# Softmax sums of a whole attention stage in one tile, with one reciprocal, one turn and one store per stage, and a block's rows asked for ahead of its weights

## The chip, the core and the metric

One core of a Trainium2 chip runs the whole program. The metric is the device time of one execution in microseconds (us), the median of several runs. Engines in this text: PE is TensorE, DVE is VectorE, ACT is ScalarE, POOL is GpSimd, and SP is the sync engine, whose queue issues most of the DMA transfers here.

## What is computed

Two transformer blocks of two layers each run one after the other, on 1024 tokens with a model width of 1024 (the first block has 256 context tokens beside them). Almost all of the reference lies outside the change. What matters is softmax attention with heads of 64 values, and the projection that mixes all heads:

```python
def one_block(qi):                                  # the other attentions have this form too
    s = jnp.einsum('bqgrd,bsgd->bgrqs', qi, keys).astype(jnp.float32)
    p = jax.nn.softmax(s, axis=-1).astype(vals.dtype)
    return jnp.einsum('bgrqs,bsgd->bqgrd', p, vals)
...
mixed = jnp.concatenate([_merge(out_fox), _merge(out_sb), _merge(out_mla), _merge(out_mem)], axis=-1)
y = jnp.einsum('bsc,cd->bsd', mixed * jax.nn.silu(gate), w_out[l])
h_res = _layer_norm_2(DEEPNORM_ALPHA_2 * h_res + y, ln_g[l], ln_b[l])
```

The first block's attention has 6 heads over all tokens and 4 heads over a neighbourhood with a bias. The second block's has 4 heads with a forget term (causal), 4 with longer queries and keys (causal), and 4 over a memory of 256 tokens.

## The kernel before

The program is a row of stages, each an own block of instructions for all engines; a stage begins when every engine has ended the one before it. Each of the four layers has an attention stage (`attention`) and, behind it, a stage that mixes and projects (`mixed_out`). They hand data over in DRAM: `YCM` holds the heads' outputs before they are divided by their softmax sums (channels by tokens), `RCP` holds one divided by those sums (heads by tokens).

**attention.** The work is cut into groups: one head and up to four blocks of 128 queries. A group passes through these steps: PE multiplies queries by keys into PSUM (`an_s`, lines 2582 to 2592); DVE adds the mask and takes the row maximum (`an_p`, L2727); ACT takes the exponential in place and leaves the row sum in `total` (L2653); PE turns the probabilities (`an_t`, L2600) and DVE or ACT copies them to SBUF (L2738, L2660); PE weighs the values (`an_oacc`, L2628); DVE takes the reciprocal of the group's sums (L2744) and copies the output (`an_oT`, L2745); SP stores both. The sums lie along the partitions, queries down, so the store of a group's reciprocals to `RCP` (L2548) writes 4 x 128 pieces of four bytes each, one for every partition and query block (2 x 128 in a group of two query blocks). There are 98 groups in the four stages (30, 20, 24, 24), 88 of them with four query blocks and 10 with two.

Every engine works through a list of its own in a fixed order. The class `Order` makes the lists: it places each step by a table of estimated costs and needs. On SP's list the loads of a head's queries (`an_q`, L2517), keys (`an_k`, L2526) and values (`an_vT`, L2529) stand between the groups' stores. DVE's list has a step `prep` for each head (L2710, L2711) that rounds keys and queries; it waits until the head's loads have landed, and all of DVE's later steps wait behind it. The last thing on SP's list is a wait for the last stores (L2551).

**mixed_out.** For each block of 128 tokens, `load(t)` on SP's list asks for the rows of `YCM`, `RCP` (spread over 64 partitions, L2820), the gates, and the residual rows. POOL multiplies rows by reciprocals (`divided`, L2902), ACT and DVE apply the gate (L2856, L2976, L2981), ACT rounds (L2865), POOL takes the rest that rounding leaves (`lower`, L2907), PE multiplies by the weights (L2960 to L2962 for the first block of tokens, L2948 to L2950 for the others), and DVE, POOL and ACT add the residual and normalise. The weights come in four parts of 1 MB (L2836), each rounded by ACT (L2878) and split by DVE (L3017). ACT's list begins

```python
weights(0)
tanh(0)
upper(0)
for k in range(1, NK // 2):
    weights(k)
```

and DVE's list begins with its share of `weights(0)`, then `gated(0)`. SP asks for `weights(0)` first, waits until POOL has set `mo_rcp` to one (`whole`, L2921), and then runs `load(0)`. In block two, where two of the eight tiles of 128 channels need no division, `divided` multiplies all eight.

Of the kernel before, what the change touches and what calls it, by code (L numbers as in the profile page):

```python
# [22 lines left out]
ALU = mybir.AluOpType  # L23
# [3 lines left out]
P = 128  # L27
DM = 1024
# [2206 lines left out]
class Order:  # L2235
# [49 lines left out]
    def parts(self):  # L2285
# [17 lines left out]
        for m, x in enumerate(self.scores):  # L2303
# [9 lines left out]
            work["exp", x] = ({"ACT": 0.42 + 0.0009 * w}, [("max", x)] + ([("out", n - 4)] if n >= 4 else []), 0.1)  # L2313
# [73 lines left out]
def attention(core, heads, kvs):  # L2387
# [31 lines left out]
    tg, pv, oo = core.counter("an_p_turned"), core.counter("an_pv"), core.counter("an_o_out")  # L2419
    given_back = {"ACT": core.counter("an_given_act"), "DVE": core.counter("an_given_dve")}  # L2420
    with ExitStack() as s:
# [12 lines left out]
        total = core.sb(s, "an_sum", [P, 4, 4])  # L2434
        rcp = core.sb(s, "an_rcp", [P, NOUT, 4])
# [56 lines left out]

        def stores_of(n):

            return 1 + min(2, len(spec[n]))

        def stored_to(n):

            return 16 * sum(stores_of(i) for i in range(n % NOUT, n + 1, NOUT))
# [5 lines left out]
        with nc.Block() as block:  # L2505

            @block.sync
            def _(sp):
                sp.wait_ge(zeroed.sem, zeroed.nth(3))
                for kind, x in o.on["SP"]:  # L2510
# [28 lines left out]
                    if kind == "store":  # L2539
# [7 lines left out]
                        with nc.allow_non_contiguous_dma(reason="a vector across partitions"):  # L2547
                            sp.dma_start(core.t["RCP"][row // HD, first:first + k * P].rearrange("(j p) -> p j", p=P), rcp[:, u, 0:k]) \  # L2548
                                .then_inc(stored[u].sem, 16)
                for n in range(max(0, NG - NOUT), NG):  # L2550
                    sp.wait_ge(stored[n % NOUT].sem, stored[n % NOUT].after(0) + stored_to(n))  # L2551

            @block.tensor
            def _(pe):
# [10 lines left out]
                for kind, x in o.on["PE"]:  # L2565
# [45 lines left out]
                    if kind == "weigh":  # L2611
# [18 lines left out]
                        ins.then_inc(pv.sem, 1)  # L2630

            @block.scalar
            def _(act):
                for kind, x in o.on["ACT"]:
# [11 lines left out]
                    if kind == "exp":  # L2646
# [46 lines left out]
            def _(dve):  # L2693
# [5 lines left out]
                for kind, x in o.on["DVE"]:  # L2699
# [39 lines left out]
                    if kind == "out":  # L2739
# [4 lines left out]
                        V_.reciprocal(rcp[:, u, 0:k], total[:, n % 4, 0:k])  # L2744
                        V_.tensor_copy(OT[:, u, 0:(k + 1) // 2 * P], O[:, 0:(k + 1) // 2 * P]).then_inc(oo.sem, 1)  # L2745
    counts = [(zeroed, 3), (hi, len(heads)), (lo, len(heads)), (lk, sum(opens)), (au, aug_no[-1]), (vt, vturns_to(len(kvs) - 1)), (qk, NS), (mxs, NS), (mx, NS),
              (ex, NS), (tg, len(o.turns)), (pv, len(o.weighs)), (oo, NG), (neg, int(any_bias)), (given_back["ACT"], o.given["ACT"]),
# [987 lines left out]
```

## Time and profile before

| | us |
|---|---|
| median of 3 runs | 4927.67 (4921.95 to 4930.57) |
| the profiled execution: its own time | 4925.49 |
| its span, first to last instruction | 4923.5 |
| PE busy / DVE busy | 4045.0 / 2709.8 |
| ACT busy / POOL busy | 1538.9 / 1588.0 |
| mean granted TensorE clock | 0.91 of full |
| DMA packets, and of them under 512 B | 621770, 200252 |

Busy times overlap, since the engines run beside each other. A "wait" below is time in which an engine had nothing to do, put down to what ended it. The start of a stage can be seen by its first instructions: the attention stages begin at 1040.35, 2554.95, 3596.94 and 4515.24 us, the stages that mix at 1448.61, 2930.94, 3880.47 and 4798.47 us.

### The profile page before, as it was taken

How to read it: one execution, taken by the hardware profiler on the slowest of the kernel's cores; microseconds unless marked ns; L12 is line 12 of the kernel's file. 1: busy time of each engine (PE TensorE's matmuls, PEld its weight loads, DVE VectorE, ACT ScalarE, POOL GpSimd, SP SyncE). 2: the span in 40 equal slices, each digit the busy share in tenths (PEclk: the TensorE clock that was granted, in tenths of full speed). 3: DMA queues.
4: the chain of work that ended last, by engine and by line, in shares of the span. 5: the costliest groups of instructions: out<-in, count | busy, mean ns of one | idle time of the engine just before them, and what ended most of it. 6: DMA issues, size and time to landing. Idle time of an engine off the chain costs nothing. (4 is left out here: it accounts for less than half of the span.)

```text
span 4923.5 us, 106002 instructions
## 1 busy us (share of the span) xinstructions
PE 4045.0 (82%) x44120; PEld 3163.1 (64%) x44120; DVE 2709.8 (55%) x4560; ACT 1538.9 (31%) x2705; POOL 1588.0 (32%) x1248
## 2 busy tenths in 40 slices
PE   6999788868878899879868877798777679968667
PEld 4887688735556677678846656686345468844446
DVE  3464455455547366545555546755644475566446
ACT  1232233234432133223225432201453320035432
POOL 2232244310016333244411105752321255413115
PEclk8999899979989899999989888799888789989889
DMA  6455433252445545543342446333134643331447
GB/s 192 145 196 189 128 80 87 69 205 33 68 105 163 167 168 190 185 107 80 80 146 45 66 93 194 121 106 114 58 63 47 145 145 115 101 116 41 54 41 204
DMA packets 621770, 572.40 MB, mean 116 GB/s; under 512 B 200252, under 2 KB 519516, under 8 KB 619284
## 3 DMA queue, kind: packets, MB, share of 16 engines
q1 hardware_dynamic: 493780, 488.22, 37.2%
q10 hardware_dynamic: 127616, 78.95, 5.6%
q8 instruction: 265, 4.34, 0.4%
q14 instruction: 109, 0.89, 0.1%
HBM read 378.80 MB, written 192.42 MB: 116 GB/s over the span
## 5 line engine op out<-in xcount | busy, mean ns | idle before, releaser
L1096 PE MATMUL pr_acc<-hH,pr_wh 128*128 128x512 f32 (+1 forms) x1288 | 483.1, 375 | 0.0
L1097 PE MATMUL pr_acc<-hL,pr_wh 128*128 128x512 f32 (+1 forms) x1288 | 466.1, 362 | 0.0
L1098 PE MATMUL pr_acc<-hH,pr_wl 128*128 128x512 f32 (+1 forms) x1288 | 466.0, 362 | 0.0
L2653 ACT ACTIVATE an_p<-an_p,an_stat 128x1280 f32<-128x1280 f32 (+5 forms) x372 | 339.7, 914 | 286.6 <-DVE an_stat L2731 274.7
L2600 PE MATMUL an_t<-ident,an_p 128*128 128x128 f32 x2152 | 331.1, 292 | 88.1 <-DVE an_pT L2738 51.6
L2686 POOL TENSOR_TENSOR an_kl<-an_k,an_kh 128x1280 fp32r<-128x1280 f32 (+3 forms) x36 | 78.5, 2180 | 1003.2 <-DVE an_qh L2711 1003.2
L2600 PEld LDWEIGHTS an_t<-ident,an_p 128*128 128x128 f32 x2152 | 252.6, 148 | 165.9 <-DVE an_pT L2738 59.0
L2628 PE MATMUL an_oacc<-an_pT,an_v 128*64 128x256 f32 (+1 forms) x2352 | 311.1, 391 | 42.1 <-DVE an_oT L2745 19.4
L2727 DVE CUSTOM_DVE_ANT_0 an_p<-an_s,an_mask 128x256 f32<-128x256 f32 (+8 forms) x308 | 275.0, 893 | 114.1 <-PE an_s L2583 63.9
L1465 POOL TENSOR_TENSOR sp_sl<-sp_w,sp_sh 128x512 fp32r<-128x512 f32 x172 | 246.2, 1438 | 200.0 <-DVE sp_sh L1540 181.6
L2004 DVE TENSOR_TENSOR rk_tu<-rk_tu,rk_ps 128x512 f32<-128x512 f32 x300 | 188.9, 683 | 194.4 <-PE rk_ps L1828 194.4
L1140 POOL TENSOR_TENSOR pr_wl<-pr_w,pr_wh 128x1024 fp32r<-128x1024 f32 x58 | 142.9, 2463 | 471.0 <-DVE pr_wh L1160 471.0
L2065 POOL TENSOR_TENSOR rk_ml<-rk_g,rk_lmask 128x256 f32<-128x256 f32 x300 | 211.0, 731 | 257.6 <-PE rk_ps L1814 256.7
L1374 PE MATMUL sp_acc<-sp_ch,sp_sh 128*128 128x512 f32 x728 | 285.8, 393 | 7.6 <-POOL sp_sl L1465 7.6
L1375 PE MATMUL sp_acc<-sp_cl,sp_sh 128*128 128x512 f32 x728 | 285.3, 392 | 0.0
L1376 PE MATMUL sp_acc<-sp_ch,sp_sl 128*128 128x512 f32 x728 | 285.1, 392 | 0.0
L1096 PEld LDWEIGHTS pr_acc<-hH,pr_wh 128*128 128x128 f32 x1288 | 246.2, 191 | 57.8 <-issue 20.7
L2660 ACT COPY an_pT<-an_t 128x512 f32<-128x512 f32 (+3 forms) x348 | 180.7, 534 | 322.3 <-PE an_t L2600 314.5
L2738 DVE COPY an_pT<-an_t 128x512 f32<-128x512 f32 (+3 forms) x264 | 163.3, 626 | 204.3 <-PE an_t L2600 198.3
L1097 PEld LDWEIGHTS pr_acc<-hL,pr_wh 128*128 128x128 f32 x1288 | 245.9, 191 | 38.1 <-issue 1.2
L1098 PEld LDWEIGHTS pr_acc<-hH,pr_wl 128*128 128x128 f32 x1288 | 245.0, 190 | 38.0
L2582 PE MATMUL an_s<-an_kh,an_qh 128*128 128x256 f32 (+2 forms) x564 | 208.1, 379 | 62.6 <-DVE an_stat L2731 46.5
(376 smaller groups left out, 9894.3 us busy)
## 6 DMA issues: line engine op xcount, KB each, us to landing
CHK<-ri_out SPq DMA_DIRECT2D x24, 1920.0 KB, 8.1
rk_in<-CHK SPq DMA_DIRECT2D x240, 128.0 KB, 2.4
pr_w<-in_w_in ACTq DMA_DIRECT2D x58, 512.0 KB, 4.3
UT<-pr_out SPq DMA_DIRECT2D x45, 640.0 KB, 4.6
sp_w<-in_w_in ACTq DMA_DIRECT2D x50, 512.0 KB, 5.2
U<-sp_c SPq DMA_DIRECT2D x100, 256.0 KB, 2.0
mod_w<-in_w_mod SPq DMA_DIRECT2D x16, 1024.0 KB, 8.3
mo_w<-in_w_out SPq DMA_DIRECT2D x16, 1024.0 KB, 9.0
```

Of the source, the lines that this page charges most:

```text
L1096: nc.tensor.matmul(out, wh[:, u, k, 0:m], hi, start=(k == 0), stop=False)
L1097: nc.tensor.matmul(out, wh[:, u, k, 0:m], lo, start=False, stop=False)
L1098: ins = nc.tensor.matmul(out, wl[:, u, k, 0:m], hi, start=False, stop=(k == KT - 1))
L1374: nc.tensor.matmul(to, sH[:, a, k, :], cH[:, i, k, :], start=(k == 0), stop=False)
L1375: nc.tensor.matmul(to, sH[:, a, k, :], cL[:, i, k, :], start=False, stop=False)
L1376: ins = nc.tensor.matmul(to, sL[:, a, k, :], cH[:, i, k, :], start=False, stop=(k == H - 1))
L1465: g.tensor_tensor(sL[:, slot(q, i)], weight(q, i), sH[:, slot(q, i)], ALU.subtract).then_inc(w_lo.sem, 1)
L2065: return nc.gpsimd.tensor_tensor(out, G[:, b % 2, g, :, :, 0, :], lm[:, :, lv:lv + 1, :].to_broadcast([P, 2, 2, CH]), ALU.mult)
L2600: ins = nc.tensor.transpose(bank[:, j * P:(j + 1) * P], Pm[:, n % NPM, j, col:col + P], ident[:])
L2628: ins = nc.tensor.matmul(to, V[:, c % 2, blocks[n][k], :], by_query(PT[:, buffer(n, k), :], a)[:, part, :], start=(k == 0), stop=(k == len ...
L2653: nc.scalar.activation(row, row, ACT.Exp, bias=stat[:, n % NPM, j, 1:2], scale=heads[groups[n][0]].scale, accum_out=total[:, n % 4, j:j + ...
L2727: V_.tensor_tensor_reduce(out=Pm[:, n % NPM, j, 0:width], in0=scores_at(m, width), in1=extra, scale=1.0, scalar=-3.0e38, op0=ALU.add, op1= ...
```

## The change

In `attention`, `total` becomes one tile with a column for every head and query block of the stage (NT columns: 100 and 80 in the first block's two layers, 96 in the second block's). ACT's exponential writes its sum there, and no longer waits for the output copy of four groups earlier. The reciprocal and the store of each group go. At the end of the stage DVE takes one reciprocal of the whole tile, PE turns it to NT x 128, DVE copies it out of PSUM, and SP stores NT rows of 512 bytes to `RCP`, which now has a row for each head in the order of the stage. In `mixed_out`, the setting to one goes, with SP's wait for it; `load(0)` is asked for ahead of `weights(0)`; and `divided` multiplies the tiles that have sums alone, in one instruction for each range of them.

```diff
-            work["exp", x] = ({"ACT": 0.42 + 0.0009 * w}, [("max", x)] + ([("out", n - 4)] if n >= 4 else []), 0.1)
+            work["exp", x] = ({"ACT": 0.42 + 0.0009 * w}, [("max", x)] , 0.1)
...
-        total = core.sb(s, "an_sum", [P, 4, 4])
-        rcp = core.sb(s, "an_rcp", [P, NOUT, 4])
+        q_first = min(sp_[0][0] for sp_ in spec)
+        NT = len(heads) * (TT // P - q_first if any_bias else SEQ // P)
+        total, rcp, rcpT = core.sb(s, "an_sum", [P, NT]), core.sb(s, "an_rcp", [P, NT]), core.sb(s, "an_rcpT", [NT, P])
...
+        def sum_column(n, j):
+            return groups[n][0] * (NT // len(heads)) + spec[n][j][0] - q_first
...
         def stores_of(n):
-            return 1 + min(2, len(spec[n]))
+            return min(2, len(spec[n]))
...
-                        with nc.allow_non_contiguous_dma(reason="a vector across partitions"):
-                            sp.dma_start(core.t["RCP"][row // HD, first:first + k * P].rearrange("(j p) -> p j", p=P), rcp[:, u, 0:k]) \
-                                .then_inc(stored[u].sem, 16)
+                sp.wait_ge(rc.sem, rc.nth(3))
+                sp.dma_start(core.t["RCP"][0:len(heads), q_first * P:q_first * P + NT // len(heads) * P], rcpT[:]) \
+                    .then_inc(sums_out.sem, 16)
...
+                sp.wait_ge(sums_out.sem, sums_out.after(1))
...
+                pe.wait_ge(rc.sem, rc.nth(1))
+                eng, count = o.back[o.uses[-2]]
+                pe.wait_ge(given_back[eng].sem, given_back[eng].nth(count))
+                nc.tensor.transpose(T2[0:NT, len(o.uses) % 2 * 512:len(o.uses) % 2 * 512 + P], rcp[:], ident[:]).then_inc(rc.sem, 1)
...
-                        if n >= 4:
-                            act.wait_ge(oo.sem, oo.nth(n - 3))
-                                             accum_out=total[:, n % 4, j:j + 1]).then_inc(ex.sem, 1)
+                                             accum_out=total[:, sum_column(n, j):sum_column(n, j) + 1]).then_inc(ex.sem, 1)
...
-                        V_.reciprocal(rcp[:, u, 0:k], total[:, n % 4, 0:k])
                         V_.tensor_copy(OT[:, u, 0:(k + 1) // 2 * P], O[:, 0:(k + 1) // 2 * P]).then_inc(oo.sem, 1)
+                dve.wait_ge(ex.sem, ex.nth(NS))
+                V_.reciprocal(rcp[:], total[:]).then_inc(rc.sem, 1)
+                dve.wait_ge(rc.sem, rc.nth(2))
+                V_.tensor_copy(rcpT[:], T2[0:NT, len(o.uses) % 2 * 512:len(o.uses) % 2 * 512 + P]).then_inc(rc.sem, 1)
...
+                load(0)
                 weights(0)
-                sp.wait_ge(whole.sem, whole.nth(1))
-                load(0)
...
-                    nc.gpsimd.tensor_tensor(yt_in[:, u], yt_in[:, u], rb[:, u], ALU.mult).then_inc(yn.sem, 1)
+                    for j0, j1, _ in summed_tiles:
+                        ins = nc.gpsimd.tensor_tensor(yt_in[:, u, j0:j1], yt_in[:, u, j0:j1], rb[:, u, j0:j1], ALU.mult)
+                    ins.then_inc(yn.sem, 1)
...
-                nc.gpsimd.memset(rb[:], 1.0).then_inc(whole.sem, 1)
...
-                  lambda tok: dst[at(tok, P), :], T["U2"], [(0, 2), (4, 8)])
+                  lambda tok: dst[at(tok, P), :], T["U2"], [(0, 2, 0), (4, 8, 4)])
```

Apart from what is added and taken away, every engine's list stands in the order in which it stood. The first place is on SP's list in the first attention stage, where the seventh head's loads stand behind three groups' stores (`an_q`, `an_k`, `an_vT`: queries, keys, values; `YCM<-an_oT`: outputs; `RCP<-an_rcp`: reciprocals). Before:

```order
L2546 DMA YCM<-an_oT 64x2x128
L2546 DMA YCM<-an_oT 64x256
L2548 DMA RCP<-an_rcp 128x4x1
L2546 DMA YCM<-an_oT 64x128 x2
L2548 DMA RCP<-an_rcp 128x2x1
L2517 DMA an_q<-UT 64x1280 x2
L2526 DMA an_k<-UT 64x1280 x2
L2529 DMA an_vT<-UT 64x1280
```

And now:

```order
L2552 DMA YCM<-an_oT 64x2x128
L2552 DMA YCM<-an_oT 64x256
L2552 DMA YCM<-an_oT 64x128 x2
L2523 DMA an_q<-UT 64x1280 x2
L2532 DMA an_k<-UT 64x1280 x2
L2535 DMA an_vT<-UT 64x1280
```

The loads now stand behind the stores of outputs alone; this repeats at each head of all four stages. The second place is the end of the same stage and the start of `mixed_out` on SP's list (`mo_w`: weights, `mo_ycm`, `mo_rcp`, `mo_gate`, `mo_yT`, `mo_x`: what `load(0)` asks for). Before:

```order
L2546 DMA YCM<-an_oT 64x256
L2548 DMA RCP<-an_rcp 128x4x1
L2505 UNCONDITIONAL_BRANCH
L2810 UNCONDITIONAL_BRANCH
L2836 DMA mo_w<-in_w_out 128x2x1024
L2816 DMA mo_ycm<-YCM 128x5x128
L2820 DMA mo_rcp<-RCP 64x5x128 x2
L2823 DMA mo_gate<-UT 128x3x128
L2823 DMA mo_gate<-UT 128x2x128
L2829 DMA mo_yT<-YG 128x3x128
L2833 DMA mo_x<-in_XC 128x1024
L2836 DMA mo_w<-in_w_out 128x2x1024 x3
```

And now:

```order
L2552 DMA YCM<-an_oT 64x256
L2554 DMA RCP<-an_rcpT 100x128
L2511 UNCONDITIONAL_BRANCH
L2822 UNCONDITIONAL_BRANCH
L2828 DMA mo_ycm<-YCM 128x5x128
L2832 DMA mo_rcp<-RCP 64x5x128 x2
L2835 DMA mo_gate<-UT 128x3x128
L2835 DMA mo_gate<-UT 128x2x128
L2841 DMA mo_yT<-YG 128x3x128
L2845 DMA mo_x<-in_XC 128x1024
L2848 DMA mo_w<-in_w_out 128x2x1024 x4
```

The first part of the weights has moved behind all that `load(0)` asks for. The third place is the end of the stage on DVE's list (`an_pT`: turned probabilities, `mo_wl`: the rest of the weights after rounding). Before:

```order
L2744 RECIPROCAL an_rcp<-an_sum 128x4
L2745 COPY an_oT<-an_oacc 128x256
L2738 COPY an_pT<-an_t 128x512 x3
L2744 RECIPROCAL an_rcp<-an_sum 128x4
L2745 COPY an_oT<-an_oacc 128x256
L2505 UNCONDITIONAL_BRANCH
L2969 UNCONDITIONAL_BRANCH
L3017 TENSOR_TENSOR mo_wl<-mo_w,mo_wh 128x2048
```

And now:

```order
L2753 COPY an_oT<-an_oacc 128x256
L2747 COPY an_pT<-an_t 128x512 x3
L2753 COPY an_oT<-an_oacc 128x256
L2755 RECIPROCAL an_rcp<-an_sum 128x100
L2757 COPY an_rcpT<-an_t 100x128
L2511 UNCONDITIONAL_BRANCH
L2981 UNCONDITIONAL_BRANCH
L3029 TENSOR_TENSOR mo_wl<-mo_w,mo_wh 128x2048
```

The small reciprocals are gone, and one of 100 columns and the copy of the turned tile stand behind the last output copy.

## Rows read from the trace of the kernel before

**Rows 1.** Busy times of the four attention stages together, with the columns of this view.
```profile
core 0: us, PE busy (x) PEld busy (x) DVE busy (x) ACT busy (x) POOL busy (x), PEclk, DMA share, GB/s
...
sum 1351.01, PE 1005.73 PEld 730.49 DVE 664.76 ACT 580.27 POOL 206.06; mean PE 251.43 PEld 182.62 DVE 166.19 ACT 145.07 POOL 51.52
```

**Rows 2.** DVE's waits for loads, each stage's start left out: total, times, longest.
```profile
DVE an_kh L2710 <- DMA an_vT<-UT: 46.6, 5, 13.1
DVE an_qh L2711 <- DMA an_q<-QK: 7.9, 2, 4.0
...
DVE an_kh L2710 <- DMA an_vT<-UT: 37.6, 5, 12.7
DVE an_qh L2711 <- DMA an_q<-QK: 9.0, 2, 8.8
...
DVE an_kh L2710 <- DMA an_vT<-KV: 24.3, 4, 7.6
DVE an_kh L2710 <- DMA an_vT<-MKV: 22.4, 3, 9.2
DVE an_kh L2710 <- DMA an_vT<-U: 4.9, 1, 4.9
...
DVE an_kh L2710 <- DMA an_vT<-KV: 29.1, 4, 9.4
DVE an_kh L2710 <- DMA an_vT<-MKV: 19.1, 3, 7.3
DVE an_kh L2710 <- DMA an_vT<-U: 9.7, 1, 9.7
```

**Rows 3.** SP's timeline at two heads' loads: start, length, instruction.
```profile
1087.03 1.10 SPq L2517 DMA_DIRECT2D an_q<-QK  x2
...
1198.09 0.59 SPq L2548 DMA_DIRECT2D RCP<-an_rcp  x1
1198.73 1.70 SPq L2517 DMA_DIRECT2D an_q<-UT  x2
```

**Rows 4.** DVE's timeline at the same two heads: start, length, wait before it.
```profile
1096.35 0.83 DVE L2710 CAST an_kh<-an_k 128x1280 fp32r<-128x1280 f32 x1 [0.26 <-DMA an_vT<-UT]
...
1217.20 0.83 DVE L2710 CAST an_kh<-an_k 128x1280 fp32r<-128x1280 f32 x1 [10.34 <-DMA an_vT<-UT]
```

**Rows 5.** Windows of 2 us during the same two heads' loads; the columns are those of rows 1.
```profile
1090.00:1092.00 2.00, 1.52 (x9) 0.82 (x9) 1.01 (x4) 1.31 (x6) 0.00 (x0) 1.00 1.02 236
1202.00:1204.00 2.00, 2.00 (x14) 1.70 (x13) 0.00 (x0) 0.99 (x5) 0.00 (x0) 1.00 0.60 44
1210.00:1212.00 2.00, 0.00 (x0) 0.00 (x0) 0.00 (x0) 0.00 (x0) 0.00 (x0) 0.84 0.80 238
```

**Rows 6.** SP's waits: for `RCP` at the stages' ends, and for a store of `stick_breaking`.
```profile
SPq L2551 <- DMA RCP<-an_rcp: 34.2, 8, 7.7
...
SPq L3137 <- DMA YCM<-sb_oT: 1.7, 1, 1.7
```

**Rows 7.** The small reciprocals by shape, first stage: busy, mean ns.
```profile
L2744 DVE RECIPROCAL an_rcp<-an_sum 128x4 f32<-128x4 f32 x20 | 3.5, 177 | 6.6 <-PE an_oacc L2628 5.6 <-remote 0.9
...
L2744 DVE RECIPROCAL an_rcp<-an_sum 128x2 f32<-128x2 f32 x10 | 1.6, 162 | 0.8 <-PE an_oacc L2628 0.4 <-issue 0.3
```

**Rows 8.** The last group's stores of outputs on SP, first attention stage.
```profile
1437.95 1.25 SPq L2546 DMA_DIRECT2D YCM<-an_oT  x2
```

**Rows 9.** The first `mixed_out`: weights landed, gates landed, first and second product.
```profile
1454.98 1.90 ACT L2878 CAST mo_wh<-mo_w 128x2048 fp32r<-128x2048 f32 x1 [18.95 <-DMA mo_w<-in_w_out]
1458.92 0.74 ACT L2856 ACTIVATE mo_tanh<-mo_gate 128x640 f32<-128x640 f32 x1 [2.05 <-DMA mo_gate<-UT]
...
1465.70 0.79 PE L2960 MATMUL mo_ps<-mo_wh,mo_yh 128*128 128x512 f32 x1 [10.00 <-POOL mo_yl L2907]
...
1480.87 0.50 PE L2948 MATMUL mo_ps<-mo_wh,mo_yh 128*128 128x512 f32 x1 [1.64 <-POOL mo_yl L2907]
```

**Rows 10.** The division on POOL in block two, over the program: busy, mean ns.
```profile
L2902 POOL TENSOR_TENSOR mo_ycm<-mo_ycm,mo_rcp 128x1024 f32<-128x1024 f32 x16 | 38.3, 2395 | 34.5 <-DMA mo_gate<-U 34.5
```

More of the change, by code:

```diff
@@ L2419, in attention @@
     tg, pv, oo = core.counter("an_p_turned"), core.counter("an_pv"), core.counter("an_o_out")
+    rc, sums_out = core.counter("an_reciprocals"), core.move("an_sums_stored")
     given_back = {"ACT": core.counter("an_given_act"), "DVE": core.counter("an_given_dve")}
@@ L2743, in _ @@
                             dve.wait_ge(stored[u].sem, stored[u].after(0) + stored_to(n - NOUT))
-                        V_.reciprocal(rcp[:, u, 0:k], total[:, n % 4, 0:k])
                         V_.tensor_copy(OT[:, u, 0:(k + 1) // 2 * P], O[:, 0:(k + 1) // 2 * P]).then_inc(oo.sem, 1)
+                dve.wait_ge(ex.sem, ex.nth(NS))
+                V_.reciprocal(rcp[:], total[:]).then_inc(rc.sem, 1)
+                dve.wait_ge(rc.sem, rc.nth(2))
+                V_.tensor_copy(rcpT[:], T2[0:NT, len(o.uses) % 2 * 512:len(o.uses) % 2 * 512 + P]).then_inc(rc.sem, 1)
     counts = [(zeroed, 3), (hi, len(heads)), (lo, len(heads)), (lk, sum(opens)), (au, aug_no[-1]), (vt, vturns_to(len(kvs) - 1)), (qk, NS), (mxs, NS), (mx, NS),
-              (ex, NS), (tg, len(o.turns)), (pv, len(o.weighs)), (oo, NG), (neg, int(any_bias)), (given_back["ACT"], o.given["ACT"]),
+              (ex, NS), (tg, len(o.turns)), (pv, len(o.weighs)), (oo, NG), (rc, 3), (sums_out, 1), (neg, int(any_bias)), (given_back["ACT"], o.given["ACT"]),
               (given_back["DVE"], o.given["DVE"])] + [(loaded[u], 16 * sum(per[u::NQB])) for u in range(NQB)]
@@ L2816, in load @@
                     sp.dma_start(yt_in[:, u], T["YCM"][0:nt * P, tok:tok + P].rearrange("(k p) t -> p k t", p=P)).then_inc(y_in.on(u), 16)
-                    for j0, j1 in summed_tiles:
+                    for j0, j1, h0 in summed_tiles:
                         for a in range(2):
-                            row = T["RCP"][2 * j0 + a:2 * j1:2, tok:tok + P].unsqueeze(0).to_broadcast([HD, j1 - j0, P])
+                            row = T["RCP"][h0 + a:h0 + 2 * (j1 - j0):2, tok:tok + P].unsqueeze(0).to_broadcast([HD, j1 - j0, P])
                             sp.dma_start(rb[a * HD:(a + 1) * HD, u, j0:j1, :], row).then_inc(y_in.on(u), 16)
@@ L3030, in mixed_out @@
           + [(yg_in, nblk if ncm else 0)] + [(stored[u], (nblk + NZ - 1 - u) // NZ) for u in range(NZ)]
-          + [(x, nblk) for x in (y_hi, y_lo, th, gm, yn, yt, mm, z_ok, st, pw, nb, nrm, sc, fin)]
-          + [(whole, 1)])
+          + [(x, nblk) for x in (y_hi, y_lo, th, gm, yn, yt, mm, z_ok, st, pw, nb, nrm, sc, fin)])
 def first_attention(core, last):
@@ L3075, in block_one @@
         mixed_out(core, l, toks, NPAIR, [(R_AG, 3), (R_NG, 2)], T["w_out"][l], ln, (conditions, [int(t < CTX // P) for t in toks]),
-                  lambda tok: xs[at(tok, P), :], lambda tok: xo[at(tok, P), :], T["UT"], [(0, 5)])
+                  lambda tok: xs[at(tok, P), :], lambda tok: xo[at(tok, P), :], T["UT"], [(0, 5, 0)])
 def stick_breaking(core, pairs, q, k, v, dst):
@@ L3661 @@
     "MOD": (2, 2, 3 * DM), "UT": (N1, TT), "CHK": (6, 6, P, TT), "EC": (NPAIR, P, 2, NCH), "VT": (RW, TT), "BON": (RW, TT),
-    "YR": (2, RW, TT), "YG": (RW, TT), "QK": (512, TT), "YCM": (DM, TT), "RCP": (DM // HD, TT),
+    "YR": (2, RW, TT), "YG": (RW, TT), "QK": (512, TT), "YCM": (DM, TT), "RCP": (12, TT),
     "SKEW": (60, GRID * P), "BIAS": (4 * GRID, 15 * GRID), "XA": (TT, DM), "XB": (TT, DM), "HA": (SEQ, DM), "HB": (SEQ, DM),
```

2 lines of the change are left out of this document (1 added, 1 removed).

## The prediction

> **What bounds the kernel now.** I read the page for the shares first, then the attention stages by themselves, since most of the edits lie there. The four last 1351.0 us together, in which PE is busy for 1005.7 and DVE for 664.8 [rows 1], so neither engine is full. The view of who waited for whom tells where the rest goes. Leaving out the start of each stage, where the first loads have to come whatever is done, DVE's step that rounds a new head's keys and queries waits for that head's loads 46.6 + 7.9 us in the first stage, 37.6 + 9.0 in the second, 24.3 + 22.4 + 4.9 in the third and 29.1 + 19.1 + 9.7 in the fourth: 210.6 us in 30 waits, up to 13.1 us each [rows 2]. DVE works through its list in order, so maxima, copies of turned tiles and output copies all stand behind such a wait, and PE, two scores ahead at most, soon stands too. These waits are the largest thing in the stages that is not work.
>
> Why do loads take so long? Two heads of the first stage show it. One head's loads are asked for from 1087.03 on [rows 3] and DVE starts on them at 1096.35, after a wait of 0.26 us [rows 4]: 9.3 us from the first request. Another's, of the same size, are asked for from 1198.73 on, right behind a store to `RCP` at 1198.09 [rows 3], and DVE starts at 1217.20, after 10.34 us of waiting [rows 4]: 18.5 us. While the first loads run, the DMA engines move 236 GB/s with a busy share of 1.02. Four us into the second they move 44 GB/s with a share of 0.60, and twelve us in they are back at 238 [rows 5]: for some ten us the transfers are under way and hardly move, and meanwhile PE runs out of work (busy 0.00 at 1210, its clock on the way from 2.4 to 1.2 GHz, 0.84 of full over that window). What is different is the store ahead. It writes pieces of four bytes, one for each partition and query block, in all 88 x 512 + 10 x 256 = 47616 over the kernel.
>
> That such a store is slow to land is seen where something waits for it alone. At the ends of the four stages SP waits for `RCP` 34.2 us in total, that is 8.6 a stage, while a store of `stick_breaking` to `YCM`, in long rows, is waited for 1.7 us [rows 6]. So a small store of reciprocals takes over 8 us to land although it holds 2 KB, and the length agrees with the ten us in which the loads behind it crawl.
>
> **The change part by part.** *The stores of each group go.* If they are what holds the loads up, the loads land in the 9.3 us of the free case. DVE reached the step of 1217.20 some 8.1 us after the first request (18.5 less 10.34), and the request itself comes earlier, because the store's 0.59 us of issue goes. A residue of about 1 us can stay in the worst five of the 30; I take 5 us in all. So 210.6 - 5 = 205.6 us less. I count a us of DVE's wait as a us of the stage. It could be less (PE has a score or two in hand when DVE stops) or more: PE's clock, which falls in such a gap, comes back only some time after work does. Ends: nothing, if something else causes the crawl; and about 240 if the clock gives back one or two us at each of some 20 longer gaps.
>
> *The final wait.* 34.2 us of waits at the ends become four like the 1.7 us of the long rows: -27.4 [rows 6]. Ahead of it stands the new chain behind the last output copy. A reciprocal took 162 ns for two columns and 177 for four [rows 7], 7.5 ns a column, so 100 columns take about 162 + 98 x 7.5 = 0.9 us; a turn and a copy of 128 columns, three hand-overs between engines beside them, I estimate at another 0.9. Meanwhile SP issues the two output stores in 1.25 us [rows 8], so some 0.5 us of the 1.8 shows: +2 for four stages. Bounds: nothing, and all of 1.8 and as much again, +14. Together -25.4.
>
> *98 small reciprocals go from DVE.* They are pipelined ahead of the copy, and where PE waits for the copy each is worth about 0.1 us: between 0 and 10; I take -2. What hides the rest is DVE's own slack. ACT's wait for the output of four groups before is not among the waits shown for it, and it goes at no gain. The order of all lists stays.
>
> *mixed_out, rows ahead of weights.* This is the part that can cost. Now the first weights are there at 1454.98 and are rounded while the rows still come; the gates are there at 1458.92; the first product starts at 1465.70 [rows 9]. Afterwards the rows come first, but ACT's list still begins with `weights(0)` and DVE's with its half of it, so both engines stand until the weights, now behind 1.6 MB of rows, are there. The two transfers together end at about the same time as now, near 1459. From there the chain has the rounding of 1.9 us on ACT [rows 9] and the split on DVE in it, which now lie beside the rows' transfer; a little is won back because POOL's multiplication is done by then. I put the first product 2 to 3 us later. But the second product waits for `load(1)` anyhow (1.64 us at 1480.87 [rows 9]), so one us a stage comes through: +4. Against it, POOL's division in block two, 2395 ns for eight tiles [rows 10], becomes two instructions for six, about 0.5 us less in a loop in which DVE's gating waits for POOL: five blocks in each of two stages, -5 at most. The setting to one cost little, since weights filled the wait. And the first weights now start into a DMA that no store is holding up. I take 0 for the four stages, from -10 to +14 (3 us at each plus rounding).
>
> Sum: -205.6 - 25.4 - 2 + 0 = -233.0. From the profiled execution's 4925.5 that is 4692.5; the median of the runs lies 2.2 higher, so 4694.
>
> **A price from the Trainium skill.** In rows 5 the trouble outlasts the store by some ten us. The Trainium skill, DMA: Bandwidth & Descriptors, section Why small descriptors are slow (HBM only), explains slowness of small pieces by fixed overhead per packet and descriptor. By that rule the store would cost its own packets' time and nothing after; that is the second rival, priced there from rows. The same page's Specifications say that below 512 bytes the DMA does a read-modify-write. This fits a slow landing; that it also stops reads behind it, the page does not say.
>
> **The rivals.**
> *The main case:* loads and final waits are both freed, 4694, with 4650 to 4760 as its own range. For it speak the pair of rows 3 to 5 and the final waits. Chance 0.78.
> *Half of it:* output stores with pieces of 512 bytes hold the loads up too, or new waits appear when the stage runs faster (the bias loads of the first block come right behind the values, PE becomes full). Half of 205.6 is kept: 4694 + 103 = 4797. Chance 0.09.
> *The small stores cost only their own packets:* each load behind one comes about a us earlier (the issue of 0.59 [rows 3] and its packets), 30 us, and the ends give 25.4 all the same, since the wait there is for the store itself: 4927.7 - 30 - 25.4 - 2 = 4870. Against it: a fixed cost per packet doesn't leave a later load at 44 GB/s four us after the store was issued. Chance 0.05.
> *Nothing of the crawl goes:* loads crawl after any store of outputs, because of the tensor they write, and the final wait was for the outputs too. Then only the 2 us of DVE are left: about 4925. Chance 0.05.
> *Slower:* as the last, and the later first weights come through in full, 3 us at each of four stages, and the new chain with its bound of 14: 4927.7 + 12 + 14 = 4953. It decides if the stores give back less than 26 us. Chance 0.03.
>
> **How the numbers follow.** The likeliest case gives 4694. Its own ends, 4650 (waits fully gone and the clock back) and 4760 (a third of the waits stays), hold nearly all of its 0.78; to leave out no more than two in ten the range reaches up into the second case, to 4785. Within 0.2% (10 us, about what a measurement of this kernel can tell from no change) lies the fourth case: 0.04; slower by more 0.03; faster 0.93.
>
> **What would show each step right or wrong.** Right: DVE's waits for `an_vT` and `an_q` behind each stage's start sum to under 20 us; windows behind a store of outputs move over 200 GB/s; SP's final wait is under 3 us a stage; PE's granted clock over an attention stage rises, and the last two stages become shorter by over 50 us each. Wrong, if loads still take over 15 us behind a store of outputs. In `mixed_out` the round of the first weights on ACT starts some 3 us later behind the stage's start than now, and the first product 2 to 3 us later. The number fails if the waits go but PE's own work turns out to need the time.

## The result, and the profile after

| | before | after |
|---|---|---|
| median, us | 4924.81 (4917.67 to 4930.57) | 4638.88 (4636.86 to 4640.08) |
| ratio | | 0.942, 95% interval 0.9403 to 0.9436 |
| profiled execution: span | 4923.5 | 4636.3 |
| mean granted TensorE clock | 0.910 | 0.936 |
| the four attention stages, sum | 1352.5 | 1066.2 |
| PE busy in them | 1007.0 | 939.1 |

The kernel became 286 us faster. The prediction said 233 faster, and its range ended at 4650, 11 us above what was measured. Here and below only fast runs are counted; two executions of the kernel before, of 5930 and 10615 us on the last of the chips used below, are left out. The attention stages hold the difference: from PE's first instruction in each to its first in the stage behind, they took 408.6, 376.4, 283.9 and 283.6 us before, and now 346.3, 322.2, 199.0 and 198.7. Outside them the trace shows two small shifts that cancel: what runs ahead of the first attention stage, which the change doesn't touch, ended 5.0 us earlier, and the four stretches behind attention stages took 3.9 us more in all. The view of busy times over these four stretches of the kernel after, with the columns of [rows 1]:

```profile
1035.10:1381.40 346.30, 306.26 (x2145) 221.84 (x2145) 211.11 (x434) 179.50 (x333) 52.97 (x17) 0.97 0.27 62
2487.90:2810.10 322.20, 288.04 (x1985) 210.57 (x1985) 196.78 (x356) 165.07 (x281) 53.02 (x17) 0.95 0.27 64
3478.90:3677.90 199.00, 172.43 (x1165) 126.30 (x1165) 127.04 (x394) 116.18 (x275) 50.25 (x24) 0.95 0.34 80
4312.60:4511.30 198.70, 172.41 (x1166) 126.43 (x1166) 126.95 (x394) 116.21 (x275) 50.26 (x24) 0.95 0.34 80
sum 1066.20, PE 939.14 PEld 685.15 DVE 661.88 ACT 576.97 POOL 206.50; mean PE 234.78 PEld 171.29 DVE 165.47 ACT 144.24 POOL 51.63
```

Against [rows 1], whose stretches begin a third of a us later, DVE's work is 3 us less, as the small reciprocals would have it. PE's same matrix work takes 68 us less, since the clock granted to it (PEclk) is 0.95 to 0.97 of full instead of 0.91, 0.89, 0.80 and 0.82. The other 218 of the 286 us were time in which PE stood.

DVE's waits for loads over the whole kernel after (total, times, longest), to be held against [rows 2] and, in each stage, its start:

```profile
DVE an_kh L2719 <- DMA an_vT<-UT: 31.8, 9, 10.3
DVE an_kh L2719 <- DMA an_vT<-U: 27.8, 4, 8.8
```

With 2.8 us for queries alone that is 62.4 us, and 50.8 of it lie at the starts of stages. Behind the starts only this is left, in the first and in the second stage:

```profile
DVE an_kh L2719 <- DMA an_vT<-UT: 7.2, 4, 3.4
...
DVE an_kh L2719 <- DMA an_vT<-UT: 4.4, 3, 2.7
```

11.6 us in 7 waits where there were 210.6 in 30: 199.0 are gone. The head of [rows 3] that waited 10.34 us [rows 4] reads so now, on SP's timeline, on DVE's, and in two windows while it loads:

```profile
1184.00 1.10 SPq L2523 DMA_DIRECT2D an_q<-UT  x2
1185.21 1.18 SPq L2532 DMA_DIRECT2D an_k<-UT  x2
1186.43 0.60 SPq L2535 DMA_DIRECT2D an_vT<-UT  x1
```

```profile
1193.75 0.83 DVE L2719 CAST an_kh<-an_k 128x1280 fp32r<-128x1280 f32 x1 [1.47 <-DMA an_vT<-UT]
```

```profile
1186.00:1188.00 2.00, 2.00 (x13) 1.25 (x14) 1.36 (x7) 2.00 (x6) 0.00 (x0) 1.00 1.05 259
1188.00:1190.00 2.00, 1.76 (x14) 1.44 (x14) 0.41 (x1) 0.76 (x3) 0.00 (x0) 1.00 1.04 228
```

The request is 9.75 us ahead of DVE's step, not 18.5, and from two to six us into it the DMA engines move 259 and 228 GB/s, where they moved 44 four us into it [rows 5].

The end of the first attention stage on DVE, PE and SP, in order of time:

```profile
1377.46 0.42 DVE L2753 COPY an_oT<-an_oacc 128x256 f32<-128x256 f32 x1 [1.97 <-PE an_oacc L2635]
1377.80 0.77 DVE L2755 RECIPROCAL an_rcp<-an_sum 128x100 f32<-128x100 f32 x1
1377.91 1.25 SPq L2552 DMA_DIRECT2D YCM<-an_oT  x2
...
1378.62 0.32 PE L2641 MATMUL an_t<-ident,an_rcp 128*100 128x128 f32 x1 [1.20 <-DVE an_rcp L2755]
1378.97 0.29 DVE L2757 COPY an_rcpT<-an_t 100x128 f32<-100x128 f32 x1 [0.41 <-PE an_t L2641]
1379.29 0.42 SPq L2554 DMA_DIRECT2D RCP<-an_rcpT  x1
```

SP is done with the outputs at 1379.16 and asks for the sums at 1379.29: the new chain of reciprocal, turn and copy lies beside the issue of the outputs and shows for 0.13 us (0.04 to 0.12 in the other three stages). Then SP waits for the landing, over the four stages (total, times, longest):

```profile
SPq L2558 <- DMA RCP<-an_rcpT: 2.6, 4, 0.8
SPq L2557 <- DMA YCM<-an_oT: 2.5, 4, 0.9
```

5.1 us instead of 34.2 [rows 6].

In the first `mixed_out`, counted from its first instruction, the rows are there after 7.2 us (10.3 before), the first weights after 12.3 (6.4 before), and the first product starts after 21.7 (17.1 before) [rows 9]:

```profile
1388.64 1.53 POOL L2914 TENSOR_TENSOR mo_ycm<-mo_ycm,mo_rcp 128x640 f32<-128x640 f32 x1 [63.07 <-DMA mo_gate<-UT]
...
1393.72 1.90 ACT L2889 CAST mo_wh<-mo_w 128x2048 fp32r<-128x2048 f32 x1 [17.66 <-DMA mo_w<-in_w_out]
1395.53 0.73 ACT L2867 ACTIVATE mo_tanh<-mo_gate 128x640 f32<-128x640 f32 x1
...
1403.10 0.80 PE L2972 MATMUL mo_ps<-mo_wh,mo_yh 128*128 128x512 f32 x1 [14.19 <-POOL mo_yl L2920]
```

### The profile page after: what moved, and what is told of

Same layout as the page of the kernel before. It is cut to its first block and busy times, and to the rows that moved or that the text cites. A ratio compares the mean times of both kernels' runs of the same rounds, so it can differ in the third digit from the quotient of the medians.

```text
span 4636.3 us, 105530 instructions
## 1 busy us (share of the span) xinstructions
PE 3978.0 (86%) x44124; PEld 3117.7 (67%) x44124; DVE 2690.9 (58%) x4470; ACT 1533.4 (33%) x2705; POOL 1581.7 (34%) x1260
## 5 line engine op out<-in xcount | busy, mean ns | idle before, releaser
L2607 PE MATMUL an_t<-ident,an_p 128*128 128x128 f32 x2152 | 313.4, 282 | 36.8 <-ACT an_pT L2669 27.1
L2607 PEld LDWEIGHTS an_t<-ident,an_p 128*128 128x128 f32 x2152 | 237.6, 142 | 111.7 <-ACT an_pT L2669 51.6
L2635 PE MATMUL an_oacc<-an_pT,an_v 128*64 128x256 f32 (+1 forms) x2352 | 290.3, 372 | 6.8 <-DVE an_pT L2747 3.5
L2747 DVE COPY an_pT<-an_t 128x512 f32<-128x512 f32 (+3 forms) x264 | 162.9, 627 | 184.3 <-PE an_t L2607 182.2
```

What stands on the lines that cost most here:

```text
L2607: ins = nc.tensor.transpose(bank[:, j * P:(j + 1) * P], Pm[:, n % NPM, j, col:col + P], ident[:])
L2635: ins = nc.tensor.matmul(to, V[:, c % 2, blocks[n][k], :], by_query(PT[:, buffer(n, k), :], a)[:, part, :], start=(k == 0), stop=(k == len ...
```

## The experiments

Each time is compared with runs of the kernel before on the same chip, and three chips took part. The kernel after took 4638.9, 4638.3 and 4632.3 (again 4633.2) us on chips A, B and C, but the kernel before 4925, 4896 and 4866 to 4873. So "over after" below means over the kernel after on the same chip: 4638.3 on B, 4632.8 (the mean of its two medians) on C, or the one measured beside it. Its four attention stages took 1066.4, 1068.5, 1066.3 and 1066.7 us in the traces of these four measurements, so the stages of a run on any chip can be held against the 1066.2 above. Differences of a few us between medians are within what the runs scatter. No trace of the kernel before was taken on B or C.

**Do the small stores do it, and what in them?** To the kernel after a store behind each group's outputs is added, from a constant tile to a tensor `RC2` that nobody reads; SP and DVE wait for it as for the old one.

```diff
         def stores_of(n):
-            return min(2, len(spec[n]))
+            return 1 + min(2, len(spec[n]))
...
+                        to = core.t["RC2"][row // HD, first:first + k * P]
+                        with nc.allow_non_contiguous_dma(reason="small pieces"):
+                            sp.dma_start(to.rearrange("(j p) -> p j", p=P), ident[:, 0:k]).then_inc(stored[u].sem, 16)
```

> The kernel after, and behind the output stores of each group a store of 4 x 128 pieces of four bytes (2 x 128 in the small groups) from a constant tile to a DRAM tensor that nobody reads, waited for as the store of reciprocals was. If these stores alone make the difference, the time goes back to that of before less some 2 us of small reciprocals and whatever the rest of the change gave: 4900 to 4935 us, with DVE's waits for loads at about 260 us, the last wait of a stage at 8 us again, and PE's granted clock at 0.91. If something else in the change did it (ACT's wait, the order in mixed_out), only 98 issues of 0.6 us and the final waits come back: under 4720.

Measured on C: 4895.9 us, 1.0052 of before (1.0035 to 1.007), 263 over after; 4900 at least was expected, from the times on A. Most of DVE's waits for loads are back, 231.6 us with the starts of stages, where before has 261.8 (on A) and after 62.4:

```profile
DVE an_kh L2722 <- DMA an_vT<-UT: 81.4, 12, 11.3
...
DVE an_kh L2722 <- DMA an_vT<-KV: 50.5, 8, 11.1
DVE an_kh L2722 <- DMA an_vT<-MKV: 40.6, 6, 9.6
DVE an_kh L2722 <- DMA an_vT<-U: 40.1, 6, 8.7
...
DVE an_qh L2723 <- DMA an_q<-QK: 19.0, 8, 7.6
```

The stages' clock is back too (0.91, 0.91, 0.81, 0.81), and SP waits 32.8 us for these stores at the four ends. The four attention stages grew by 257.7 us. Nothing else in the change is needed for its gain. That it comes out some 27 us above before on that chip, where the sum of its other parts would ask for 6, stays open.

The next four change the one line, with the same 2 KB (one quarter in the last); the `.then_inc` at the end of each line is left out here:

```diff
# sixteen_bytes
+ sp.dma_start(to.rearrange("(p j) -> p j", p=P), ident[:, 0:k])
# rows_512
+ sp.dma_start(to.rearrange("(j p) -> j p", p=P), ident[0:k, :])
# spread, with RC2 of (DM // HD, TT, P) and `to` its element 0
+ sp.dma_start(to.rearrange("(j p) e -> p j e", p=P), ident[:, 0:k].unsqueeze(2))
# one_column
+ sp.dma_start(to[0:P].rearrange("(j p) -> p j", p=P), ident[:, 0:1])
```

> As four_bytes, but the same 2 KB are written as 128 pieces of 16 bytes (128 of 8 in the small groups): a quarter of the pieces. If each piece costs something and what is behind waits for all of them, the landing shrinks from some 10 us to 2.5 to 4 and about a quarter to a third of the 286 us comes back: 4700 to 4740. If a store with small pieces has a fixed price, it is as slow as four_bytes, about 4915.

> As four_bytes, but the same 2 KB are written as 4 pieces of 512 bytes, from 4 partitions (2 pieces in the small groups). If the number or the size of the pieces is what costs, only the issue of a third store per group is left: 4640 to 4660. If it is one more store behind the outputs, whatever its form: about 4915.

> As four_bytes, with 512 pieces of four bytes in each store, but each goes to a place of its own, 512 bytes from the next. If what costs is that neighbouring pieces of four bytes from different partitions hit the same stretch of DRAM, the price goes: within 20 us of rows_512. If it is the 512 pieces themselves, it is as four_bytes: some 260 us over the kernel after.

> As four_bytes, but only one query block's column in each group: 128 pieces of four bytes, a quarter of the pieces of four_bytes and as many as sixteen_bytes, each of a quarter of its size. If the number of pieces decides, it is like sixteen_bytes: within 10 us of rows_512. If a piece of four bytes as such has a price, a quarter of the way back to before: about 70 us over the kernel after. If the first such piece already has the price of all, the full 265.

And pieces of four bytes with as many to a stretch as `sixteen_bytes` has, one every 16 bytes (`RC2` of (DM // HD, TT, 4), "(p j) e -> p j e"; a store covers 8 KB, and the four pieces of a partition lie behind one another):

> As four_bytes, with 512 pieces of four bytes, each 16 bytes from the next: the addresses and the density of sixteen_bytes, but pieces of a quarter of its size and four times as many. Four-byte pieces side by side cost 203 to 258 us and pieces 512 bytes apart nothing. If it is how many pieces fall into one stretch (32 in 512 bytes, as in sixteen_bytes, in place of 128), it is free: within 10 us of spread, about 4640. If it is that pieces of less than 16 bytes share a stretch with others at all, the stores' price is back: over 4800.

| kernel (chip) | pieces in a store of four blocks | of them in 512 bytes | us | over after | SP's wait for it at an end |
|---|---|---|---|---|---|
| four_bytes (C) | 512 of 4 B, side by side | 128 | 4895.9 | 263 | 8.2 |
| one_column (B) | 128 of 4 B, side by side | 128 | 4841.1 | 203 | 7.5 |
| pitch_16 (C) | 512 of 4 B, 16 B apart | 32 | 4657.8 | 26 | 1.6 |
| sixteen_bytes (C) | 128 of 16 B, side by side | 32 | 4643.2 | 10 | 0.4 |
| spread (B) | 512 of 4 B, 512 B apart | 1 | 4639.0 | 1 | 0.6 |
| rows_512 (C) | 4 of 512 B | 1 | 4632.7 | 0 | below 0.2 |

What costs is neither the third store, nor the number of pieces, nor that a piece has four bytes: 512 such pieces cost nothing that the medians tell when each has a stretch of DRAM of its own (one run of four is 13 us over the others, and in its trace the four attention stages take 5 us more than those of after on B), and 128 cost 203 us when they are neighbours. Of the expectations only those for `spread` and `rows_512` came true (`rows_512` 7 us below its 4640, as the kernel after is on C). `sixteen_bytes` was to cost a quarter of the price or all of it, `one_column` 10, 70 or 265 us, and `pitch_16` nothing or over 160; what each was to decide is seen from the table alone. How long the stretch is, the six kernels don't tell: counted in 16, 64 or 512 bytes, the first two have four times as many pieces to a stretch as the next two. Nor was it tried whether it matters that neighbours come from different partitions, as in the first two, or from one, as in `pitch_16`. The waits for `four_bytes` and `spread`, from SP's view of waits:

```profile
SPq L2560 <- DMA RC<-ident: 32.8, 4, 8.5
```

```profile
SPq L2560 <- DMA RC<-ident: 2.5, 4, 0.9
```

**Is it only the loads behind them?** The stores of `four_bytes` in those groups alone behind which a stage loads no more heads:

```diff
+                        if x >= last_load:
+                            to = core.t["RC2"][row // HD, first:first + k * P]
...
```

> As four_bytes, but only in the groups behind the last load of a stage: 34 of 98 stores, 10 in the first stage and 8 in each other. If the small stores cost time only through the loads of heads behind them, as the prediction counted it, what comes back is the last wait of each stage, some 27 us, and 1 or 2 us of issue: 4665 to 4675. If they also hold up the outputs, their slots and the fetching of instructions as much, about a third of 286 us comes back: 4735.

Measured on C: 4678.5 us, 0.9611 of before (0.9592 to 0.963), 46 over after. DVE's waits for loads stay at 62.6 us. SP waits at the ends for the added stores and for the sums

```profile
SPq L2564 <- DMA RC<-ident: 36.7, 4, 10.6
...
SPq L2565 <- DMA RCP<-an_rcpT: 1.6, 3, 0.9
```

together 38.3 against 5.1, so 33.2 of the 43.2 us by which the stages grew are ends. 10.0 us are left for 34 stores, 0.3 us each, that no load of a head explains. That is little, but more than the 2 us by which the stages of after scatter over four traces. It isn't the issue of one more store as such: `rows_512` has 98 such issues, and its stages take 1065.1 us. The theory of loads alone is nearly right, the one of a full third refuted.

**What is a us of DVE's wait worth?** The kernel after, with DVE kept busy where it used to wait, and no transfer changed:

```diff
+HOLD = 8
...
                         V_.tensor_copy(qH[rows, u, 0:nq], qT[rows, u, 0:nq]).then_inc(hi.sem, 1)
+                        if t:
+                            for r in range(HOLD):
+                                V_.bn_stats(held_out[:, (t * HOLD + r) * 6:(t * HOLD + r + 1) * 6], mask[:, 0:512])
```

> The kernel after, in which DVE is kept busy behind the rounding of each head but a stage's first (40 in all) by eight instructions that compute statistics of a constant tile, 686 ns each by a row of the same form: 40 x 8 x 0.686 = 220 us of DVE time added where it used to wait for loads; no transfer is changed. If a us of DVE's wait is a us of the stage, as the prediction counted it, the time is 220 over the kernel after, and half or less if PE's scores in hand cover much of each hold. If the clock (and what else stands behind DVE) gives back more than the wait itself, as the rest between 233 and 286 would ask, it is 270 to 290 over, with the attention stages' granted clock below 0.90.

Measured on B: 4866.0 us, 228 over after. The sum over the four stages:

```profile
sum 1297.20, PE 1020.03 PEld 742.84 DVE 848.54 ACT 581.50 POOL 205.57; mean PE 255.01 PEld 185.71 DVE 212.14 ACT 145.38 POOL 51.39
```

The instructions overlapped each other more than a sum of their durations says, so DVE was held for 848.5 - 661.9 = 186.7 us, and the stages grew by 231.0: 1.24 us for one. PE shows both sides of it. It stood only 150.1 us longer (277.2 against 127.1), since it had scores in hand. Its own work became 80.9 us longer, with the granted clock at 0.91, 0.90, 0.82 and 0.82 in the four stages. Neither of the numbers written down fits: the one us for one came out in the total only because the hold was 187 and not 220.

The same with holds twice as long at every second head (`HOLD = 16`, `if t % 2`):

> As dve_hold, but with 16 of the instructions at every second head (22 heads, 352 instructions), so that DVE is held 9 to 10 us at a time, as long as the longer waits for loads of the kernel before (up to 13.1 us), in place of 4.7. In dve_hold DVE's busy time in the stages grew by 186.7 us, 0.583 for each instruction, and the stages by 230.9: 1.24 for each. Here DVE's busy time should grow by 205. If the price of a held us doesn't depend on the length of the hold, the stages grow by 254 and the time is 4886 to 4896. If long holds cost more because the scores in hand cover less of each, and the clock falls further, the factor is about 1.35, and the time 4910 to 4925; that would account for the 8 to 17 us of the attention stages' gain that 1.24 leaves open. If long holds cost less a us (the clock falls once and not twice), below 4870.

Measured on C: 4864.3 us, 0.9993 of before (0.9983 to 1.0003), 232 over after. The sum over its stages:

```profile
sum 1293.40, PE 981.99 PEld 715.11 DVE 869.06 ACT 579.02 POOL 205.09; mean PE 245.50 PEld 178.78 DVE 217.26 ACT 144.75 POOL 51.27
```

DVE held 207.2 us, stages 227.2 longer: 1.10. PE stood 184.3 longer, since scores in hand cover less of a long hold, but its work grew by 42.8 alone (clock 0.84 in the last two stages). The third case of the expectation came true: long holds cost less, not more, and what 1.24 leaves open grows.

**What is the turn worth?** No turn and no copy; SP stores the reciprocals as they lie.

```diff
-                sp.wait_ge(rc.sem, rc.nth(3))
-                sp.dma_start(core.t["RCP"][0:len(heads), q_first * P:q_first * P + NT // len(heads) * P], rcpT[:]) \
-                    .then_inc(sums_out.sem, 16)
+                sp.wait_ge(rc.sem, rc.nth(1))
...
+                    for h in range(len(heads)):
+                        sp.dma_start(core.t["RCP"][h, q_first * P:q_first * P + per_head * P].rearrange("(j p) -> p j", p=P),
+                                     rcp[:, h * per_head:(h + 1) * per_head]).then_inc(sums_out.sem, 16)
```

> The kernel after without the turn, its copy and the store of rows at a stage's end: SP stores the reciprocals as they lie, one store for each head (10, 10, 12 and 12), with 1024 or 1280 neighbouring pieces of four bytes each, 46 thousand over the four stages. Tells what the turn is for. Ten or twelve issues of 0.6 us beside the landing: a landing of 8 us whatever the number of pieces (7.5 us for 128 and 8.2 for 512 in one_column and four_bytes) gives four ends of some 14 us in place of 3.5, +42. If the price grows with the pieces beyond 512 by the 1.8 ns a piece of those two, 11520 pieces take 21 us more at each end: +125. If stores in a row add their 8 us each: 44 x 8 = +350.

Measured on C: 4822.3 us, 0.9911 of before (0.9889 to 0.9932), 189 over after. SP in the first stage, and its waits:

```profile
1376.63 32.67 SPq L2557 DMA_DIRECT2D RCP<-an_rcp  x10
1426.70 0.36 SPq L2825 DMA_DIRECT2D mo_ycm<-YCM  x1
```

```profile
SPq L2561 <- DMA RCP<-an_rcp: 68.2, 4, 18.0
```

Issuing alone takes 32.7 us instead of 6, then come 18. So with over a thousand pieces in a store the price does grow with them: 189 us for 47616 pieces, 4.0 ns each. None of the three numbers written down fits; the second is nearest. The turn is worth 189 us to this design, at 0.13 us a stage.

**What did the part in `mixed_out` do?** Four kernels with 5 rounds each, all on C, two beside each measurement of after. `mixed_old` is the kernel after with the old code there (one division over all eight tiles too):

```diff
+                weights(0)
+                sp.wait_ge(whole.sem, whole.nth(1))
                 load(0)
-                weights(0)
...
+                nc.gpsimd.memset(rb[:], 1.0).then_inc(whole.sem, 1)
```

> The kernel after, with mixed_out as before: the weights asked for first, the setting to one and SP's wait for it, one division over all eight tiles. The prediction valued this part of the change at 0, from 14 us of loss to 10 of gain for it; so 4639, from 4625 to 4649. In the traces the first product starts 4.6, 6.2, 2.7 and 3.2 us later behind the start of its stage than before, 16.7 us together. If that comes through in full, this kernel is some 17 us faster than after: 4622. If the second product waits for its rows anyhow, it is within 5 us of it.

`gate_first` puts the gate's steps ahead of the weights' in the lists of ACT and DVE:

```diff
-                weights(0)
                 tanh(0)
                 upper(0)
+                weights(0)
...
+                gated(0)
                 weights(0)
-                gated(0)
```

> The kernel after, in which ACT's list in mixed_out begins with the tanh and the rounding of block 0 and DVE's with its gate, ahead of the first weights, which now land last. The rows are there 7.2 to 8.5 us behind the start of the stage, the weights at 12.1 to 13.1; so the gate's chain lies beside the weights' transfer, and the first product can start at some 17 us (the rounding of 1.9 and the split of 2.3 us behind the weights) in place of 21.7 to 22.7. If that comes through: 4 x 5 = 20 us less, 4619. If the second product waits for load(1) instead: 0 to 6 us less.

Then two with the residual rows of block 0 asked for behind the last weights (`residual(0)` ahead of `load(1)`): one on top of `gate_first`, one with the weights first in all lists.

> gate_first (rows ahead of weights, the gate's steps ahead of the weights' in both lists), and the residual rows of block 0, 512 KB that only the sum needs, behind the last weights. In gate_first the first product starts 16.4 to 18.5 us behind the stage's start and waits for weights that land at 11.9 to 13.7; 512 KB less ahead of them let them land some 2 us sooner. If that comes through: 4 x 2 = 8 us less than gate_first, 17 less than after, 4616 to 4620. If the end of the first product hangs on the fourth part of the weights, it comes through as well, since they too move 2 us; if it hangs on DVE and ACT, nothing: as gate_first, 9 less than after.

> The kernel after, with the order of before (first weights, then rows, in all lists), without the setting to one and its wait, and with the residual rows of block 0 behind the last weights. In mixed_old the weights land at 5.1 and the rows at 9.5 to 11.2; without the wait for the setting to one (0.8 us) and 512 KB of residual rows the rows should land 1 to 3 us sooner, and the first product with them. 8 us less than after for the order, and 4 to 10 more for this: 12 to 18 less. If only the order of the lists cost something in the change, it is as mixed_old: 8 less.

| kernel | us | against after beside it | first product, us behind the stage's start |
|---|---|---|---|
| after | 4632.3 (4629.0 to 4639.0) | | 22.0, 22.3, 22.4, 23.3 |
| mixed_old | 4624.4 (4621.1 to 4630.1) | -7.9 | 16.3, 16.2, 19.0, 19.5 |
| gate_first | 4622.9 (4621.3 to 4626.8) | -9.4 | 16.4, 17.4, 18.5, 18.2 |
| after, again | 4633.2 (4628.8 to 4639.9) | | 21.2, 21.6, 22.6, 22.3 |
| residual_late | 4624.6 (4617.1 to 4629.4) | -8.7 | 16.4, 16.0, 18.5, 19.4 |
| weights_first | 4621.1 (4611.5 to 4637.2) | -12.2 | 16.7, 16.6, 18.4, 18.8 |

The first product of `gate_first` and what leads to it, in the first stage (start 1384.3): the rounding for it is done while the weights come.

```profile
1391.78 0.74 ACT L2867 ACTIVATE mo_tanh<-mo_gate 128x640 f32<-128x640 f32 x1 [12.84 <-DMA mo_gate<-UT]
...
1396.06 2.35 POOL L2920 TENSOR_TENSOR mo_yl<-mo_yT,mo_yh 128x1024 fp32r<-128x1024 f32 x1 [2.70 <-ACT mo_yh L2876]
1396.22 1.90 ACT L2889 CAST mo_wh<-mo_w 128x2048 fp32r<-128x2048 f32 x1 [0.24 <-DMA mo_w<-in_w_out]
...
1400.71 0.77 PE L2972 MATMUL mo_ps<-mo_wh,mo_yh 128*128 128x512 f32 x1 [10.11 <-DVE mo_wl L3029]
```

So this part of the change costs some 8 us, 4 or 5 to either side by the scatter of the runs, and it costs them through the lists: either order of the transfers gives them back if ACT and DVE take up first what lands first. For `mixed_old` and `gate_first` the time lies between the two numbers expected of each. The residual rows are worth nothing that these runs can tell. Of 5 us a stage for the first product about 2 come through. `gate_first` beats both kernels: 0.949 of before (0.9475 to 0.9506), and its slowest run is faster than the fastest of after beside it. `weights_first` is as good as far as these runs tell; its runs scatter by 26 us.

## Why the prediction was wrong

*The mechanism was right.* The stores of reciprocals held up the loads and the ends [rows 2, 5, 6]; `four_bytes` puts such stores back and the time returns. 199.0 of the 210.6 us went; the residue was put at 5 and is 11.6. The size was off in two places, and both make the gain larger.

*The step that failed is "I count a us of DVE's wait as a us of the stage".* The two biases named beside it do not cancel: the clock is the stronger one. `dve_hold` and `dve_hold_long` measure 1.24 and 1.10, so 199.0 us of waits are 219 to 247 us of stage, where the sum had 205.6. The waits of before, 7 us on average, lie between the holds of 4.7 and 9.4 us. The upper end named for it, about 240, took the clock to give back one or two us at each of some 20 gaps; PE's busy time fell by 68 us over 30 waits, a little over two each.

*A term was missing.* The crawl holds up more than the loads of heads. `tail_only` shows 0.3 us a store with no such load behind it, 29 us if it held for all 98, though much of it would lie beside the loads' waits. With the ends (29) and DVE's work (3) the sum is 251 to 279 without this term and 280 to 308 with all of it; the stages gained 286. So the rate alone falls short by 7 to 35 us. Two other runs ask for the same: the stages of `four_bytes` grew by 257.7 us and those of `one_column` by 206.6, of which 29 each are ends, and DVE's waits grew by 169.2 and 133.8; at 1.10 to 1.24 that leaves 18 to 42 and 12 to 30. How the missed 53 us divide between rate and term stays open, and so does what the term consists of. One thing more that the crawl slowed are the loads of biases (`an_bias`), which took 11.7 us from issue to landing before (median) and take 5.0 now; no engine's wait is put down to them. One reading of the views can be ruled out. In the view of waits some starts of PE's weight loads stand as "issue", ended by no engine's work. For `an_s` and `an_oacc` before (total, times, longest):

```profile
PEld an_s L2582 <- issue: 64.9, 100, 11.3
PEld an_oacc L2628 <- issue: 63.4, 180, 8.8
PEld an_s L2590 <- issue: 43.7, 33, 7.4
```

and after:

```profile
PEld an_s L2589 <- issue: 38.1, 100, 1.1
...
PEld an_oacc L2635 <- issue: 24.8, 124, 0.5
PEld an_s L2597 <- issue: 9.0, 30, 0.5
```

PE's waits of 7 to 11 us there are gone. But `dve_hold_long`, which has no small store and changes no transfer, has them all again:

```profile
PEld an_s L2593 <- issue: 76.1, 99, 10.6
PEld an_oacc L2639 <- issue: 55.6, 153, 8.9
...
PEld an_s L2601 <- issue: 45.5, 34, 9.5
```

So they come with DVE's stops, whatever stopped it, and don't show a second thing that the stores hold up.

*The final wait* was sized right: 34.2 to 5.1, so -29.1 for -27.4, and the new chain cost 0.1 a stage for the 0.5 taken. The reciprocal of 100 columns took 0.77 us for 0.9.

*The small reciprocals:* DVE's work fell by 2.9 us for the 2 taken; not tested alone.

*`mixed_out`, taken at 0,* costs 7.9 on C, inside its bounds of -10 and +14. The first product came 4.6, 6.2, 2.7 and 3.2 us later, not 2 to 3, because the weights landed 12 to 13 us behind the start, and not at the some 10 by which both transfers ended in the first stage before; ACT's rounding of them starts 6 to 7 us later, not 3. About half of the delay of the first product comes through.

*The rivals.* That small stores cost their own packets alone is refuted by 44 GB/s becoming 228 to 259. The Trainium skill, DMA: Bandwidth & Descriptors, section Why small descriptors are slow (HBM only), would have a price with each small packet; `spread` has as many as `four_bytes` and costs 1 us, so no price of this kind shows here. Its Specifications name a read-modify-write below 512 bytes. If that alone were slow, `spread`, whose pieces are of four bytes too, would be. That it takes many such writes to one stretch agrees with the six kernels, though none of them shows what the DRAM or the DMA does there. `YCM`'s pieces of 512 bytes (the half case) hold up nothing: 228 GB/s behind them.

*The size depends on the chip.* The kernel before is the one that moves, by 60 us over three chips, while after moves by 7. The gain was 286 us on the chip of the prediction's profile, 258 on B and 232 to 241 on C. A gain that hangs on how long a crawl takes is known no better than the crawl; that it is the crawl that differs was not shown, since no trace of before was taken on B or C. The 11 us by which the range missed are less than these differences, and on C the forecast of 233 would have come out almost to the us. That would have been luck: the waits that it was worked out from are A's, and there the conversion was wrong.

## What to carry to other kernels

A store of a per-partition scalar to consecutive words of DRAM held up the loads behind it for some ten us here: turn it on the chip so that each row leaves as one piece, or at least give each piece 16 bytes. When a wait of an engine that feeds the matmuls is priced, a us can be more than a us of the stage, since the clock falls too: the two rates measured here are 1.10 and 1.24. And where the order of transfers is changed, each consumer's list has to be changed with it, or the first to land waits for the last.

## What the runs showed of the hardware

Writes of four bytes to neighbouring addresses (128 in 512 bytes) landed 7.5 and 8.2 us after SP began to wait, with 128 and 512 of them in a store (`one_column`, `four_bytes`), and cost 4.0 ns a piece in stores of 1024 and 1280 (`no_turn`). 32 pieces in 512 bytes cost 26 us (`pitch_16`) and 10 (`sixteen_bytes`) in place of 263, and one in 512 bytes nothing that could be told (`spread`). The loads that suffered read other tensors. The same change gained 286, 258 and 232 to 241 us on three chips of one kind.
